# Heads' scores side by side in two attentions, a top-16 over 72 sums, and low parts of weights four groups later

## What is computed

```python
# nsa_attention, per block of 128 queries and per head: three masked softmaxes (31 compressed keys, all causal keys twice)
s = einsum('bqgrd,bcgd->bgrqc', qb, k) * scale;  p = masked_softmax(s, mask);  o = einsum(..., p, v)
# stick_breaking_attention
z = q.k * scale;  log_keep = where(mask, log_sigmoid(-z), 0)
after = reverse cumsum(log_keep) - log_keep;  a = exp(log_sigmoid(z) + after);  o = a.v
# peer_ffn, per token and each of 8 heads
s = q.sub_keys                                   # two halves of 128 keys
s_top, i_top = top_k(s, 16)                      # 16 of each half, sorted
cand = s_top[0][:, None] + s_top[1][None, :]     # 16 x 16 sums
best, pos = top_k(cand, 16)                      # the 16 best pairs, then experts = i_top0 * 128 + i_top1
g = softmax(best);  y = sum_e g_e * gelu(u_e . x) * v_e
```

## Time and profile before

| what | us |
| --- | --- |
| median of three runs | 3551.23 |
| lowest, highest | 3548.71, 3552.36 |
| the profiled execution | 3549.85 |
| its span, first to last instruction | 3548.4 |
| TensorE busy | 3301.7 (93%) |
| VectorE busy | 2273.8 (64%) |
| ScalarE busy | 1303.9 (37%) |
| GpSimd busy | 807.3 (23%) |
| mean granted TensorE clock | 0.964 of full speed |

### The profile page before, as it was taken

The page is one execution under the profiler, slowest core; times in us unless marked ns, Lnnn a source line. Parts: engine busy times, 40 slices in busy tenths (PEclk is TensorE's granted clock), DMA queues, the critical chain, the costliest instruction groups (busy, mean ns, idle before and its releaser), DMA issues. The chain is left out here.

```text
span 3548.4 us, 45109 instructions
## 1 busy us (share of the span) xinstructions
PE 3301.7 (93%) x17156; PEld 2753.9 (78%) x17156; DVE 2273.8 (64%) x4365; ACT 1303.9 (37%) x2284; POOL 807.3 (23%) x751
## 2 busy tenths in 40 slices
PE   7999989999999999997998998866889999999998
PEld 6445548888766688885776877766889999999998
DVE  4666445646455565464553336997778888888886
ACT  3333333223333332233453223225863333343433
POOL 1000341000100020004000002376853333334341
PEclk9999989999999999997998998988999999999999
DMA  3332102222211132222111222243579989899883
GB/s 136 125 108 76 51 24 89 95 102 87 93 48 42 42 107 91 100 89 69 65 35 57 90 89 83 85 159 129 211 274 316 323 309 321 308 319 316 308 313 124
DMA packets 180454, 515.17 MB, mean 145 GB/s; under 512 B 14992, under 2 KB 75408, under 8 KB 175120
## 3 DMA queue, kind: packets, MB, share of 16 engines
q1 hardware_dynamic: 128256, 305.70, 25.1%
q0 software_dynamic: 40464, 160.45, 13.2%
q10 hardware_dynamic: 11520, 46.15, 3.4%
HBM read 477.10 MB, written 35.13 MB: 144 GB/s over the span
## 5 line engine op out<-in xcount | busy, mean ns | idle before, releaser
L230 PE MATMUL bank<-h_hi,w_hi 128*128 128x512 f32 (+1 forms) x2528 | 970.4, 384 | 76.3 <-ACT w_hi L198 21.1
L230 PE MATMUL bank<-h_lo,w_hi 128*128 128x512 f32 (+1 forms) x2528 | 953.9, 377 | 0.0
L204 DVE TENSOR_TENSOR w_lo<-w_raw,w_hi 128x1024 fp32r<-128x1024 f32 (+1 forms) x468 | 599.8, 1282 | 333.5 <-ACT w_hi L198 327.6
L198 ACT ACTIVATE w_hi<-w_raw 128x1024 fp32r<-128x1024 f32 (+1 forms) x508 | 546.0, 1075 | 543.8 <-PE bank L230 526.3
L230 PEld LDWEIGHTS bank<-h_hi,w_hi 128*128 128x128 f32 x2528 | 487.9, 193 | 163.4 <-issue 48.5
L230 PE MATMUL bank<-h_hi,w_lo 128*128 128x512 f32 (+1 forms) x2528 | 596.7, 373 | 16.3 <-POOL w_lo L211 16.3
L230 PEld LDWEIGHTS bank<-h_lo,w_hi 128*128 128x128 f32 x2528 | 488.9, 193 | 67.4 <-issue 11.4
L230 PEld LDWEIGHTS bank<-h_hi,w_lo 128*128 128x128 f32 x2528 | 460.0, 189 | 86.1 <-POOL w_lo L211 17.6
L230 PE MATMUL bank<-e_hi,w_hi 128*128 128x384 f32 x1024 | 345.4, 337 | 5.9 <-DVE e_lo L2262 5.9
L230 PE MATMUL bank<-e_lo,w_hi 128*128 128x384 f32 x1024 | 344.2, 336 | 0.0
L2171 POOL DMA_INDIRECT own_row<-in_u_rows,own_e x128 | 157.9, 1233 | 321.5 <-DVE sums L2299 277.5
(11 more groups left out here) (405 smaller groups left out, 4754.1 us busy)
## 6 DMA issues: line engine op xcount, KB each, us to landing
w_raw<-in_w SPq DMA_DIRECT2D x476, 512.0 KB
ada_w<-in_ada_w POOLq DMA_DIRECT2D x24, 1024.0 KB, 5.1
expert_weights<-G ACTq DMA_DIRECT2D x12, 2048.0 KB, 7.3
Gin<-expert_weights SPq DMA_DIRECT2D x32, 768.0 KB
w_raw<-in_w SPq DMA_DIRECT2D x32, 704.0 KB
hidden_ahead<-u_stage ACTq DMA_DIRECT2D x40, 192.0 KB, 3.4
ahead<-hidden_ahead SPq DMA_DIRECT2D x20, 384.0 KB
na_bias<-in_bias ACTq DMA_DIRECT2D x4, 896.0 KB, 4.5
```

Of the source, the lines that this page charges most:

```text
L198: sc.activation(w_hi[s][:, 0:n], w_raw[raw_slot[u]][:, 0:n], ACT.Copy).then_inc(*w_hi_made.next(u))
L204: ve.tensor_tensor(w_lo[s][:, 0:n], w_raw[raw_slot[u]][:, 0:n], w_hi[s][:, 0:n], ALU.subtract).then_inc(*w_lo_made.next(u))
L230: m = te.matmul(out, wt, moving, start=(not low and k == 0 and moving is hi), stop=(low and k == len(blocks) - 1))
```

## The change

Three edits. (1) In `nsa` and `stick` TensorE's loop over heads is cut in two: first the scores of both heads, then the transposes or sums of both. (2) In `combine` the 256 sums become 72, in four blocks given by `CAND`: rows 0 and 1 with all 16 columns, rows 2 and 3 with 8, rows 4 to 7 with 4, rows 8 to 15 with one. Positions are decoded by thresholds: the column by an and with a mask made from three comparisons, the row by comparing the position with the first position of each row (a step instead of a one-hot, multiplied by differences of neighbouring indices). (3) In `scatter` VectorE's low part of a unit moves from group 6k+3 to group 6k+7, and the last one behind the loop. Waits between engines stay as they are.

```diff
+CAND = ((0, 0, 2, 16), (32, 2, 4, 8), (48, 4, 8, 4), (64, 8, 16, 1))
+N_CAND = 72
@@ nsa, tensor
                         te.matmul(s_bank[hh][:, 0:w], q[p % 2][rows, i * P:(i + 1) * P], key[rows, 0:w], start=True, stop=True).then_inc(*pe.next("nsa scores", hh, g))
+                for hh in range(2):
                     if g >= 3:
                         m2, b2, p2, i2, w2 = place(g - 3)
@@ combine
-        cand = sb(st, "cand", [P, H8, K16, K16])
+        cand = sb(st, "cand", [P, H8, N_CAND])
@@ combine, vector
-                ve.tensor_tensor(cand[:, :, :, :], v4[:, :, 0, :].unsqueeze(3).to_broadcast([P, H8, K16, K16]),
-                                 v4[:, :, 1, :].unsqueeze(2).to_broadcast([P, H8, K16, K16]), ALU.add).then_inc(*dve.next())
+                for at, lo, hi, n in CAND:
+                    ve.tensor_tensor(cand[:, :, at:at + (hi - lo) * n].rearrange("p h (a b) -> p h a b", b=n),
+                                     v4[:, :, 0, lo:hi].unsqueeze(3).to_broadcast([P, H8, hi - lo, n]),
+                                     v4[:, :, 1, 0:n].unsqueeze(2).to_broadcast([P, H8, hi - lo, n]), ALU.add).then_inc(*dve.next())
-                            cand[:, h, :, :].rearrange("p a b -> p (a b)"), work[h % 2][:, :]) for h in (h0, h0 + 1)])
+                            cand[:, h, :], work[h % 2][:, 0:N_CAND]) for h in (h0, h0 + 1)])
-                ve.tensor_scalar(part[1][:, :, :], pos[:, :, :], 15, None, ALU.bitwise_and).then_inc(*dve.next())
-                ve.tensor_scalar(part[0][:, :, :], pos[:, :, :], 4, None, ALU.logical_shift_right).then_inc(*dve.next())
+                ve.tensor_copy(partf[0][:, :, :], pos[:, :, :]).then_inc(*dve.next())
                 ve.wait_ge(*dve.here())
-                for half in (1, 0):
-                    ve.tensor_copy(partf[half][:, :, :], part[half][:, :, :]).then_inc(*dve.next())
-                    ve.wait_ge(*dve.here())
+                pf = partf[0][:, :, :].rearrange("p h k -> p (h k)")
+                for n, (at, by) in enumerate(((32, -8.0), (48, -4.0), (64, -3.0))):
+                    ve.tensor_scalar(past[n][:, :], pf, float(at), by, ALU.is_ge, ALU.mult).then_inc(*dve.next())
+                ve.tensor_copy(less[:, :, 0:1], idxf[:, :, 0, 0:1]).then_inc(*dve.next())
+                ve.tensor_tensor(less[:, :, 1:K16], idxf[:, :, 0, 1:K16], idxf[:, :, 0, 0:K16 - 1], ALU.subtract).then_inc(*dve.next())
+                ve.wait_ge(*dve.here())
+                ve.tensor_tensor(past[0][:, :], past[0][:, :], past[1][:, :], ALU.add).then_inc(*dve.next())
+                ve.wait_ge(*dve.here())
+                ve.scalar_tensor_tensor(mask[:, :, :].rearrange("p h k -> p (h k)"), past[2][:, :], 15.0, past[0][:, :], ALU.add, ALU.add).then_inc(*dve.next())
+                ve.wait_ge(*dve.here())
+                ve.tensor_tensor(part[:, :, :], pos[:, :, :], mask[:, :, :], ALU.bitwise_and).then_inc(*dve.next())
+                ve.wait_ge(*dve.here())
+                ve.tensor_copy(partf[1][:, :, :], part[:, :, :]).then_inc(*dve.next())
+                ve.wait_ge(*dve.here())
+                for half, table, how in ((1, slot16[:, K16:2 * K16], ALU.is_equal), (0, slot16[:, 0:K16], ALU.is_ge)):
                     ve.tensor_tensor(o3[half], partf[half][:, :, :].rearrange("p h k -> p (h k)").unsqueeze(2).to_broadcast([P, HK, K16]),
-                                     iota16[:, :].unsqueeze(1).to_broadcast([P, HK, K16]), ALU.is_equal).then_inc(*dve.next("places", half, i))
+                                     table.unsqueeze(1).to_broadcast([P, HK, K16]), how).then_inc(*dve.next("places", half, i))
@@ scatter, vector
-                if s == 3:
+                if s == 7:
                     ve.wait_ge(*w_lo_made.at(U[0]))
-                if s % 6 == 3:
-                    split_lo(U[s // 6] + 1)
+                if s % 6 == 1 and s >= 6:
+                    split_lo(U[s // 6 - 1] + 1)
+            split_lo(U[-1] + 1)
```

More of the change, by code:

```diff
@@ L61 @@
                   ("causal_neg", P), ("strict_t", P), ("tri", P), ("win_neg", DH), ("cmp_neg", TT * 32),
-                  ("iota", P), ("iota16", 16)):
+                  ("iota", P), ("slot16", 32)):
     TABS[_name] = _at
@@ L1908, in combine @@
         U = take(24)
-        iota16 = sb(st, "iota16", [P, K16])
-        cand = sb(st, "cand", [P, H8, K16, K16])
+        slot16 = sb(st, "slot16", [P, 2 * K16])
+        cand = sb(st, "cand", [P, H8, N_CAND])
         oh = [sb(st, f"oh{half}", [P, H8, K16, K16]) for half in range(2)]
@@ L1913, in combine @@
         pos = sb(st, "pos", [P, H8, K16], U32)
-        part = [sb(st, f"part{half}", [P, H8, K16], U32) for half in range(2)]
+        part = sb(st, "part", [P, H8, K16], U32)
         partf = [sb(st, f"partf{half}", [P, H8, K16]) for half in range(2)]
         idxf = sb(st, "idxf", [P, H8, 2, K16])
+        less = sb(st, "less_last", [P, H8, K16])
+        past = [sb(st, f"past{n}", [P, HK]) for n in range(3)]
+        mask = sb(st, "pmask", [P, H8, K16], U32)
         rs = sb(st, "prs", [P, H8])
@@ L1920, in combine @@
         whole_h = sb(st, "whole_h", [P, KT, P])
-        iota16_in = loaded("iota16_in")
+        slot16_in = loaded("slot16_in")
         def turn_res(i):
@@ L1951, in scalar @@
             after(sc, before)
-            sc.dma_start(iota16[:, :], tabs("iota16", K16)).then_inc(*iota16_in.next("in"))
+            sc.dma_start(slot16[:, :], tabs("slot16", 2 * K16)).then_inc(*slot16_in.next("in"))
             sc.preload_act_table_set("exp_and_others")
@@ L1976, in vector @@
             after(ve, before)
-            ve.wait_ge(*iota16_in.at("in"))
+            ve.wait_ge(*slot16_in.at("in"))
             ve.tensor_tensor(whole_h[:, :, :], h_hi[:, :, 0:P], h_lo[:, :, 0:P], ALU.add).then_inc(*dve.next("whole h"))
@@ L2027, in vector @@
                 ve.wait_ge(*dve.here())
-                ve.tensor_tensor(oh[0][:, :, :, :], oh[0][:, :, :, :], idxf[:, :, 0, :].unsqueeze(2).to_broadcast([P, H8, K16, K16]),
+                ve.tensor_tensor(oh[0][:, :, :, :], oh[0][:, :, :, :], less[:, :, :].unsqueeze(2).to_broadcast([P, H8, K16, K16]),
                                  ALU.mult).then_inc(*dve.next())
@@ L2036, in gpsimd @@
             after(gp, before)
-            gp.wait_ge(*iota16_in.at("in"))
+            gp.wait_ge(*slot16_in.at("in"))
             for i in range(TT):
@@ L2570, in tables @@
     put("iota", np.broadcast_to(np.arange(P, dtype=np.float32), (P, P)))
-    put("iota16", np.broadcast_to(np.arange(16, dtype=np.float32), (P, 16)))
+    first = [at + (a - lo) * n for at, lo, hi, n in CAND for a in range(lo, hi)]
+    put("slot16", np.broadcast_to(np.array(first + list(range(16)), np.float32), (P, 32)))
     return t
```

## The result

The changed kernel takes 3471.64 us (median of four, 3466.77 to 3474.5) against 3550.22; the ratio is 0.9777 (95% interval 0.976 to 0.9794; the intervals below are of the same kind), a gain of 78.6 us where 89 were forecast. The range held it.

| from | to | before, us | after, us | gain | forecast |
| --- | --- | --- | --- | --- | --- |
| start | first scores of the first attention | 90.7 | 88.7 | 2.0 | - |
| there | first scores of stick-breaking | 276.3 | 246.4 | 29.9 | 33 |
| there | last product with v | 156.9 | 141.8 | 15.1 | 15 |
| there | VectorE's first instruction of the search | 1744.8 | 1744.6 | 0.2 | 0 |
| there | first product G | 164.9 | 149.1 | 15.8 | 28 |

What follows compares the result with a forecast made beforehand. TensorE was taken to set the pace in both attentions, VectorE in the search, no engine full in the one-hot stage. 33 + 15 + 28 + 13 = 89 us off 3549.9 gives 3460.9, 3462 at the median's level; range 3440 to 3492.

Steps and rivals of the forecast that it cites:

- once per pair of heads: First attention: about 0.2 to 0.5 us may be lost to late VectorE per pair of heads; minus 1 us in all.
- the pairs' increments: First attention: semaphore increments written one after the other, some 26 ns each, would take 1.6 us off the gain.
- I had added 1.5 us for this: Stick-breaking, last four steps: at the low clock scores cost up to double, so 1.5 us more gain.
- the step from the first cast to the one-hot: Search, decoding the place: ten small operations after, some 1.35 us more per tile, 5.4 us in all.
- four instructions of 576 elements in all will be about 1.1 us plus the same collision. Saves 1.2 x 4: Search, building the sums on VectorE: four instructions replace one of 2048 elements, saving 4.8 us (nothing to 13).
- Rival B: Search bound by GpSimd and TensorE from tile 2 on: gain 15 us instead of 28, total 3475; chance 0.15.
- Rival C: One-hot stage hangs on ScalarE and GpSimd more tightly: gain 4 us instead of 13, total 3471; chance 0.10.
- catch-up: Search: GpSimd's and TensorE's chain has until tile 3's last reduction; VectorE would wait 0 to 5 us there.
- Rival D: One-hot stage: TensorE's small waits lower its granted clock from 0.99, making the kernel slower, 3603 us; chance 0.03.
- rival F: One-hot stage: VectorE's scalar one-hots hold GpSimd's, 21 us lost instead of 13 won, total 3496; chance 0.02.
- its first half and not the second: GpSimd contends with VectorE's two-input instructions (first half, borne out) and its two-port modes (second, not borne out).

Runs made afterwards that it cites:

- e1: The kernel before with only the scores of both heads side by side, in both attentions; 3501.36 us, ratio 0.9866.
- e2: The kernel before with only the 72 sums in the search; 3533.42 us, ratio 0.9952.
- e4: The changed kernel with the sums of all four tiles built at once ahead of tile 0, four instructions instead of sixteen; 3465.21 us, ratio 0.9761.
- e5: The kernel before, GpSimd forming only 128 of 1024 columns of each low part in the search (results wrong, only times used); 3533.59 us, measured once.
- e6: The changed kernel, GpSimd forming only 128 of 1024 columns of each low part in the search (results wrong, only times used); 3441.61 us, measured once.
- e7: The changed kernel with VectorE, not ScalarE, making the fourth one-hot A in one of six groups of the one-hot stage; 3462.91 us, ratio 0.9752.

## Why the prediction was right, point by point, and where not

**First attention, right term by term.** Slot by slot the gain is 0.44, 0.56, 0.77, 0.99 and 1.20 us for 31, 128, 256, 384 and 512 columns; the forecast had 0.45, 0.56, 0.77, 0.99 and 1.20. Two sizes were off: a slot loses some of it to the late VectorE "once per pair of heads", four times, but five slots do (12, 24, 36, 40, 42: 1.9 us), and the last slot gave 0.8. So 31.2 for 33. That the pairs' increments cost 1.6 us, by "TensorE: Matmul & The Clock Gate" of the Trainium skill (The cost: per-tile semaphore tail), isn't seen: the pairs take 0.01 us more than one head.

**Stick-breaking, the right number from two errors.** The other steps with filling gain at least as forecast (0.82, 1.02, 1.20 to 2.3). The first step of pairs 1 to 3 loses 1.6, 1.3 and 0.8 us where 0.56 was to be gained. One reason is a wait that was moved in front of other work. TensorE in order of time, changed kernel and then the one before:

```profile
366.32 0.66 PE L1033 MATMUL bank<-sb_q,sb_k 64*128 64x128 f32 x2
367.65 0.76 PE L1033 MATMUL bank<-sb_q,sb_k 64*128 64x128 f32 x2 [0.66 <-ACT sb_t L1077]
368.34 2.07 PE L1040 MATMUL bank<-sb_lk,tri 128*128 128x512 f32 x2
```

```profile
399.66 0.46 PE L1028 MATMUL bank<-sb_q,sb_k 64*128 64x128 f32 x2
400.48 2.07 PE L1034 MATMUL bank<-sb_lk,tri 128*128 128x512 f32 x2 [0.36 <-POOL sb_lk L1145]
```

Before, head 0's sums came 0.82 us after head 0's scores; now 2.02, behind head 1's scores and their wait (0.66 us, in the other two pairs 0.56 and 0.48). I had asked what stands behind the waiting instruction for the first attention and not for this one. The other reason is the clock. These steps begin at 1.2 GHz, and more of that falls into them now: 366.4 to 373.3 in this one, where it was 400.0 to 403.4, so that the mean granted clock of the step is 0.76 instead of 0.87 (0.76 instead of 0.83 and 0.70 instead of 0.74 in the other two). The 3.4 us more at half the clock are up to 1.7 us, an estimate, so the clock can be the larger part. e1, with the same stick-breaking code, has its low stretch from 361.2 to 368.0, most of 3 us ahead of this step. TensorE in order of time in e1:

```profile
364.09 1.01 PE L1029 MATMUL bank<-sb_q,sb_k 64*128 64x128 f32 x4
365.03 2.07 PE L1036 MATMUL bank<-sb_lk,tri 128*128 128x512 f32 x2
```

There the wait isn't seen, the sums come 0.94 us after the scores, and the three steps gain 0.4, 0.0 and 0.0 us. Where the low stretch is as long in both kernels (e2 with the old loop and e1 with the new, 6.8 us), steps 3 and 4 together gain 1.76 us, as forecast (1.20 + 0.56); the changed kernel gains 0.8 on e2. So the wait is seen in the changed kernel, where the low stretch starts with the step, and not in e1; how the loss divides between wait and clock isn't shown. Step 0 lost 1.6 as well, in 3.4 us at 1.2 GHz that e1 doesn't have there. Steps 0 to 12 together gave 5.6 us instead of 10.6 (three times 0.77, 0.99, 1.20 and 0.56). The last three gave 9.4 instead of 3.0, and the difference is the clock: before, 495.6 to 519.5 ran at 1.2 GHz; in the changed kernel it stayed at 2.4 from 448.4. Why is open: TensorE had been busy 8 of 10 us ahead of the fall in the one, and 6 to 7 of 10 where it didn't fall in the other. Windows of the last steps, before and after:

```profile
503.00:524.00 21.00, 17.07 (x38) 7.39 (x36) 7.48 (x13) 5.69 (x10) 8.53 (x16) 0.61 0.00 0
```

```profile
462.00:477.00 15.00, 10.40 (x40) 5.43 (x40) 7.47 (x13) 5.46 (x10) 8.53 (x16) 1.00 0.00 0
```

I had added 1.5 us for this. It isn't sure income: in e1, with the same stick-breaking code, 10 us of the last steps ran low, and the last took 16.6 us instead of 14.4; there the start of the stage went better, and the stage gained 15.1 all the same.

**Search, the step that failed.** Of VectorE's own work every term holds. A top-16 group starts 2.29 us after the one before (forecast 2.29); the step from the first cast to the one-hot is 2.50 us instead of 0.87, 1.64 more (forecast 1.35). What failed is "four instructions of 576 elements in all will be about 1.1 us plus the same collision. Saves 1.2 x 4". Groups by shape of the search, before and after (busy us, mean ns):

```profile
L2004 DVE TENSOR_TENSOR cand<-pvals 128x2048 f32<-128x2048 f32 x4 | 17.3, 4330 | 0.3
```

```profile
L2014 DVE TENSOR_TENSOR cand<-pvals 128x128 f32<-128x128 f32 x8 | 10.8, 1386 | 0.0
L2014 DVE TENSOR_TENSOR cand<-pvals 128x256 f32<-128x256 f32 x4 | 9.9, 2465 | 0.3
L2048 DVE TENSOR_TENSOR pres<-best 128x128 f32<-128x128 f32 x4 | 9.8, 2448 | 0.0
...
L2026 DVE CAST idxf<-pindex 128x256 f32<-128x256 uint32 x4 | 4.3, 1079 | 0.1
L2039 DVE TENSOR_TENSOR part<-pos,pmask 128x128 uint32<-128x128 uint32 x4 | 3.4, 852 | 0.1
```

With four of 64 elements (3.1 us) the builds hold 24 us: 6.7 more instead of 4.8 less, and that is 11.5 of the 12.2 us that are missing. Take each shape at its least (0.28 us for two inputs of 128 elements, 0.41 of 256, 0.21 of 64, 2.29 of 2048) and the rest is meetings: 27 us before, 41 after. Search less meetings: 164.9 - 27 = 138, 149.1 - 41 = 108, 30 us of own work gone, as forecast, and 14 of it given back. I priced a meeting per tile where it is to be priced per instruction that meets (nine of the sixteen builds).
Rival B forecast 15 for this stage, and its mechanism isn't what happened: in the changed kernel VectorE has no wait for GpSimd's or TensorE's chain, and e4, e5 and e6 shorten the stage with VectorE's held time. Rival C's 3471 us is even the measured time, and its stage came out at the other end. A total that fits is no evidence for a mechanism; the stages are. The "catch-up" of 2 us wasn't there either; it shows only in e6. And the total of this forecast fitted in part by luck: the search gave 12 us too little, the one-hot stage 5 too much (2.6 of it lost again behind it), and stick-breaking is right by two errors.

**One-hot stage.** The hole of 3 us at the fourth group is gone and ScalarE waits 1.4 us for TensorE instead of 14.4. The unit is 9.55 to 10.3 us, 10.1 in the mean, for 10.3: the lead built up at the start carries the first units at TensorE's own pace, which I had left out; so 18.2 for 13. Then 2.6 us go behind it. TensorE's wait for the first high part of the next stage, before and after:

```profile
PE bank L230 <- ACT w_hi L198: 4.8, 1, 4.8
```

```profile
PE bank L234 <- ACT w_hi L202: 7.4, 1, 7.4
```

A stage bound by ScalarE ends with ScalarE behind TensorE, and the next begins with its high part. e7 brings this wait back to 4.7. Rival D (lower clock) isn't borne out, 0.99 in both; F isn't, GpSimd's one-hots take 0.756 us in the mean, before 0.771.

## What to carry to other kernels

Where VectorE and GpSimd both work in SBUF, count instructions before elements: a small one of VectorE beside a long one of GpSimd costs the rest of that one, mostly 2.4 us here, so merge small builds (here four for sixteen, 6 us). A product moved from GpSimd to the full VectorE cost nothing here, and gained nothing. When a loop is cut in two to set like matmuls side by side, list for each half what now stands behind which wait. And when a wait's removal makes another engine the bound, look at how that engine enters the next stage.

## What the runs showed of the hardware

Beside a two-input instruction of GpSimd not only VectorE's two-input ones are held but also casts (1.68 us for 0.30, and in e4 one of 4.74 beside two of GpSimd), copies (2.38 for 0.17) and scalar operations (2.4 for 0.22). MAX8, FIND_INDEX8, MATCH_REPLACE8 and TENSOR_REDUCE took their usual time, within 0.03 us, in every run: the reduce at 2251.35 took its usual 2.29 us beside a low part of 2250.36 to 2253.56. In the prediction I said of "GPSIMD Engine Reference" of the Trainium skill (Key points) that the trace bears out its first half and not the second, two-port modes; for the search that was wrong, since one-input instructions are held there (in which mode they run, no trace shows). The trace of the kernel before had it already, VectorE and then GpSimd in order of time:

```profile
2369.85 2.43 DVE L2019 CAST partf<-part 128x128 f32<-128x128 uint32 x1
```

```profile
2368.58 3.62 POOL L211 TENSOR_TENSOR w_lo<-w_raw,w_hi 128x1024 fp32r<-128x1024 f32 x1 [2.20 <-ACT w_hi L198]
```

The scalar one-hots of the one-hot stage are another kind: 0.33 us at the least for 128 elements, where the scalar operations of the search take 0.22 alone, and GpSimd's one-hots beside them took 0.60 at the median as before, so rival F stayed away. The page "Trainium Architecture — The Big Picture" of the Trainium skill (What this means for kernel authors) calls the shared port an exclusive lock and not a split of bandwidth. The trace agrees: three builds and three GpSimd instructions in turns, and 7.42 us for four builds. GpSimd pays, too: its products take 2.4 us alone and 4.4 in a meeting, 3.4 in the mean.
